# One level of Strassen's algorithm in the output projection of a hybrid decoder layer

## What is computed

```
h = rms_norm(x, norm_mix)
y_mix, xq = gla_branch(h, ...)                  # (2048, 1024), (2048, 512)
y_mem = memory_cross_attention(xq, m, w_kv)     # (2048, 512)
x = x + concatenate([y_mix, y_mem], -1) @ w_out # w_out is (1536, 1024): the product that is changed
x = x + (relu(rms_norm(x, norm_mlp) @ w_up) ** 2) @ w_down
return rms_norm(x, final_norm)
```

## Time and profile before

| what | value |
|---|---|
| median of 3 runs | 2588.22 us (2587.95 to 2590.2) |
| the profiled execution | 2587.02 us, of which the span in the trace is 2585.2 us |
| mean granted clock of PE | 0.998 of full |
| busy: PE, PEld | 2533.5 us (98%), 2118.9 us (82%) |
| busy: DVE, ACT, POOL | 1536.7 us (59%), 1205.3 us (47%), 452.9 us (18%) |
| DMA | 338.96 MB, mean 131 GB/s |

### The profile page before, as it was taken

The page is one execution under the profiler, slowest core; times in us unless marked ns, Lnnn a source line. Parts: engine busy times, 40 slices in busy tenths (PEclk is TensorE's granted clock), DMA queues, the critical chain, the costliest instruction groups (busy, mean ns, idle before and its releaser), DMA issues.

```text
span 2585.2 us, 34664 instructions
## 1 busy us (share of the span) xinstructions
PE 2533.5 (98%) x11968; PEld 2118.9 (82%) x11968; DVE 1536.7 (59%) x2253; ACT 1205.3 (47%) x1752; POOL 452.9 (18%) x411
## 2 busy tenths in 40 slices
PE   7999999999999999999999999999999999999998
PEld 6888887888788888888878888888887888888886
DVE  4457467665656636566646664656665565465666
ACT  4544344544454525455454443544445444354544
POOL 4144444000004510000001541000000254000000
PEclk9999999999999999999999999999999999999999
DMA  8522468444522132543442213255443222344443
GB/s 284 156 90 66 158 208 286 173 129 147 181 66 71 61 114 82 195 147 131 137 158 66 82 50 114 98 179 163 146 136 126 66 66 77 103 136 158 147 161 132
DMA packets 191896, 338.96 MB, mean 131 GB/s; under 512 B 7041, under 2 KB 119041, under 8 KB 183521
## 3 DMA queue, kind: packets, MB, share of 16 engines
q1 hardware_dynamic: 188784, 327.92, 38.3%
q10 hardware_dynamic: 2928, 8.66, 0.8%
HBM read 311.39 MB, written 25.17 MB: 130 GB/s over the span
## 4 chain that ended last, share of the span: by engine, by line
issue 49%; PE 40%; DVE 4%; POOL 4%; ACT 2%; DMA 1%; SPq 1%; DVEq 0%; ACTq 0%; POOLq 0%
PE banks L1593 10%; PE banks L1595 10%; PE banks L1594 10%; PE banks L1749 3%; PE banks L1729 1%; POOL queries L700 1%; DVE w_lo L1122 1%; POOL h_lo L725 1%; PE banks L1790 1%; PE banks L1773 1%; PE banks L1788 1%; POOL rstd L658 1%; DVE u_lo L1500 1%; ACT w_hi L761 1%; DVE sr L1332 0%
## 5 line engine op out<-in xcount | busy, mean ns | idle before, releaser
L1593 PE MATMUL banks<-h_hi,w_hi 128*128 128x512 f32 (+1 forms) x1728 | 667.5, 386 | 10.6 <-DVE w_lo L1122 3.6
L1595 PE MATMUL banks<-h_hi,w_lo 128*128 128x512 f32 (+1 forms) x1728 | 659.1, 381 | 0.0
L1594 PE MATMUL banks<-h_lo,w_hi 128*128 128x512 f32 (+1 forms) x1728 | 659.0, 381 | 0.0
L1122 DVE TENSOR_TENSOR w_lo<-raw,w_hi 128x2048 fp32r<-128x2048 f32 x144 | 349.2, 2425 | 297.7 <-ACT w_hi L761 297.7
L761 ACT ACTIVATE w_hi<-raw 128x2048 fp32r<-128x2048 f32 x144 | 275.5, 1913 | 269.6 <-PE banks L1593 230.1
L1593 PEld LDWEIGHTS banks<-h_hi,w_hi 128*128 128x128 f32 x1728 | 324.9, 188 | 77.1 <-issue 16.3
L1595 PEld LDWEIGHTS banks<-h_hi,w_lo 128*128 128x128 f32 x1728 | 324.8, 188 | 63.2
L1594 PEld LDWEIGHTS banks<-h_lo,w_hi 128*128 128x128 f32 x1728 | 325.0, 188 | 60.7
L1593 PE MATMUL banks<-w_hi,u_hi 128*128 128x512 f32 x896 | 351.8, 393 | 0.0
L1595 PE MATMUL banks<-w_hi,u_lo 128*128 128x512 f32 x896 | 349.1, 390 | 0.0
L1594 PE MATMUL banks<-w_lo,u_hi 128*128 128x512 f32 x896 | 348.8, 389 | 0.0
(11 more groups left out here) (170 smaller groups left out, 3224.3 us busy)
## 6 DMA issues: line engine op xcount, KB each, us to landing
raw<-in_w_up SPq DMA_DIRECT2D x64, 1024.0 KB, 5.4
raw<-w_mix SPq DMA_DIRECT2D x64, 1024.0 KB, 4.8
raw<-in_gla_w_in SPq DMA_DIRECT2D x57, 1024.0 KB, 5.0
raw<-in_w_down SPq DMA_DIRECT2D x48, 1024.0 KB, 4.7
raw<-in_w_out SPq DMA_DIRECT2D x24, 1024.0 KB, 5.0
xin<-in_x SPq DMA_DIRECT2D x5, 2048.0 KB, 10.9
xin<-in_w_down SPq DMA_DIRECT2D x10, 1024.0 KB, 4.9
w_mix<-xin SPq DMA_DIRECT2D x10, 1024.0 KB, 10.3
```

Source lines behind the costliest of these rows:

```text
L1122: nc.vector.tensor_tensor(w_lo[:, i % 2, :], raw[:, i % 2, :], w_hi[:, i % 2, :].bitcast(F32), ALU.subtract).then_inc(lo_split.sem, PIECES)
L1593: after_chunk(pe.matmul(to, left[0], right[0], start=start, stop=False, skip_group_check=goes_on))
L1594: pe.matmul(to, left[0], right[1], start=False, stop=False, skip_group_check=goes_on)
L1595: return pe.matmul(to, left[1], right[0], start=False, stop=stop, skip_group_check=goes_on)
```

## The change

The output projection of a block is written as the product of a left side of 512 tokens by 1536 and w_out, each cut in halves both ways. The inner halves are not contiguous: the first holds y's p = 0 and the memory's heads 0 and 1, the second y's p = 1 and heads 2 and 3. Seven products of 256 tokens (two pairs of tiles), 6 slices and 512 columns take the place of eight: 84 products a block. Each is cut into a part "m" (2 slices, memory) and a part "y" (4 slices):

```diff
-OUT_ORDER = (2, 0, 1)
-C_MLP = C_OUT + 6
+OUT_CHUNKS = [(("M1", "m"), ("M5", "m")), (("M1", "y"),), (("M2", "m"),), (("M2", "y"),), (("M5", "y"),),
+              (("M6", "m"),), (("M6", "y"),), (("M3", "m"), ("M7", "m")), (("M7", "y"),), (("M3", "y"),),
+              (("M4", "m"),), (("M4", "y"),)]
+C_MLP = C_OUT + len(OUT_CHUNKS)
...
+OUT_BANKS = {"M1": 2, "M6": 2, "M7": 2, "M4": 2, "M5": 4, "M3": 4, "M2": 6}
+ORDERED = {"M2": "M1", "M3": "M6", "M7": "M5"}
+Y_LOWS = [(0, 0), (1, 0), (0, 1), (1, 1), (2, 1), (3, 1)]
...
-MIX_STEPS = UPS
-MIX_EARLY = 6
-MIX_IN_OUT = 8
+OUT_MIX = 6
+MIX_STEPS = OUT_MIX + UPS
+MIX_EARLY = 9
+MIX_IN_OUT = 11
```

```diff
+                        C_OUT + 6: [(mix_load, 9), (mix_load, 10)], C_OUT + 9: [(mix_store, 9), (mix_load, 11)],
+                        C_OUT + 11: [(mix_store, 10), (mix_load, 12)], C_MLP: [(mix_store, 11), (mix_load, 13)],
...
-                    if i == C_OUT + 3:
+                    if i == C_OUT + 4:

                         sp.wait_ge(*read(n, ("oT", TILES - 1, 1)))
                         sp.dma_start(xres[:, :, :], x_tiles[:, bass.ds(x_row, TILES), :])\
```

The left sums of the memory's values are ten sums of 128x512 on POOL, one behind each of the half steps 5 to 14 of the recurrence. Those of y are four sums of 128x1024 on POOL, behind `su` of the last chunk, as their place in memory is that of the q and the states. ACT copies each sum to fp32r, DVE subtracts:

```diff
+            def mem_sums(n, step):
...
+                if behind is not None:
+                    pool.wait_ge(*mem_sum_step.at(n, behind))
+                nc.gpsimd.tensor_tensor(to, a, b, op).then_inc(mem_sum_step.sem, 1)
...
+                def y_sums():
...
+                    pool.wait_ge(*full(n, ("su", TILES - 1, 1)))
+                    nc.gpsimd.tensor_tensor(s3, a11, a21, ALU.subtract).then_inc(y_sum_ready.sem, 1)
+                    pool.wait_ge(*read(n, ("oT", TILES - 1, 1)))
+                    nc.gpsimd.tensor_tensor(s1, a21, a22, ALU.add).then_inc(y_sum_ready.sem, 1)
+                    pool.wait_ge(*y_sum_ready.at(n, 1))
+                    nc.gpsimd.tensor_tensor(s2, s1, a11, ALU.subtract).then_inc(y_sum_ready.sem, 1)
+                    pool.wait_ge(*y_sum_ready.at(n, 2))
+                    nc.gpsimd.tensor_tensor(s4, a12, s2, ALU.subtract).then_inc(y_sum_ready.sem, 1)
...
                 end_products(n, TILES - 1)
                 o_rsqrt(TILES - 1)
-                for p in range(2):
-                    for c in range(TILES):
-                        y_low(c, p)
+                for c, p in Y_LOWS[:4]:
+                    y_low(c, p)
+                y_sums()
+                for c, p in Y_LOWS[4:]:
+                    y_low(c, p)
```

DVE's order in the stage (`y_sum_low(S1)` waits for the sum S2 as well, since it writes over what S2 reads):

```diff
+                for c, p in Y_LOWS[2:4]:
+                    gate_output(c, p)
                 next_chunk(C_OUT + 1)
+                for c in (2, 3):
+                    for p in range(2):
+                        gate_output(c, p)
                 update_state(TILES - 1)
-                for c in range(TILES):
-                    gate_output(c, 1)
+                mem_sum_low(S4)
+                mem_sum_low(S3)
...
+                next_chunk(C_OUT + 2)
+                y_sum_low(S1)
+                next_chunk(C_OUT + 3)
+                y_sum_low(S2)
+                dve.wait_ge(*xres_loaded.at(n, 0))
+                add_product("M1")
+                y_sum_low(S4)
+                next_chunk(C_OUT + 4)
+                add_product("M2")
+                y_sum_low(S3)
+                next_chunk(C_OUT + 5)
+                add_product("M5")
...
+                add_product("M3")
+                split_lo_piece(n, C_OUT + 11, 1)
+                for t in range(2):
+                    norm_ms(0, t)
+                for t in range(2):
+                    norm_scale(0, t, xres, hn)
+                next_chunk(C_OUT + 11)
+                add_product("M4", (0,))
+                norm_ms(0, 2)
                 h_low(0, 0)
+                add_product("M4", (1,))
```

PE's order. M1 and M5 "m" are out_part(C_OUT, 0) and (C_OUT, 1):

```diff
+                out_part(C_OUT, 0)
+                pieces_done[0] = 1
+                output_transposes(0, 0)
+                output_transposes(1, 0)
+                out_part(C_OUT, 1)
+                pieces_done[0] = 1
                 state_step("o", TILES - 1)
+                output_transposes(0, 1)
+                output_transposes(1, 1)
+                out_part(C_OUT + 1, 0)
+                pieces_done[0] = 1
+                output_transposes(2, 0)
+                output_transposes(2, 1)
+                out_part(C_OUT + 1, 1, (0,))
+                output_transposes(3, 0)
+                output_transposes(3, 1)
+                out_part(C_OUT + 1, 1, (1,))
+                pieces_done[0] = 1
                 state_step("kT", TILES - 1)
+                out_chunk(C_OUT + 2)
                 state_step("su", TILES - 1)
...
+                for i in range(C_OUT + 3, C_MLP - 1):
+                    out_chunk(i)
```

More of the change, by code:

```diff
@@ L256, in state_uses @@
         for p in range(2):
-            yield (6 + p if last else 3 - p), ("su", c, p)
+            yield (p if last else 3 - p), ("su", c, p)
     elif what == "o":
@@ L515, in y_row, with row_of, out_piece_of, is_half @@
             return scratch[:, c, :] if c < 2 else y_rows[:, c - 2, :]
+        def row_of(c, p):
+            return late_rows[:, c, :] if p else y_row(c)
+        def out_piece_of(i, piece):
+            parts = OUT_CHUNKS[i - C_OUT]
+            name, part = parts[piece] if len(parts) > 1 else parts[0]
+            return name, part, 2 * piece if part == "y" else 0
+        def is_half(i):
+            return C_OUT <= i < C_MLP and OUT_CHUNKS[i - C_OUT][0][1] == "m" and len(OUT_CHUNKS[i - C_OUT]) == 1
+        def out_source(name, part):
+            operand = OPERANDS_OF[name][1]
+            if operand >= T1:
+                return w_out_mix[:, operand - T1, 0:4, :] if part == "y" else w_out_mix[:, operand - T1, 4:6, :]
+            row, col = {B11: (0, 0), B21: (1, 0), B22: (1, 1)}[operand]
+            first, count = (4 * row, 4) if part == "y" else (KD + 2 * row, 2)
+            return wout[:, first:first + count, 512 * col:512 * (col + 1)]
         def last_piece(i):
@@ L590, in load_block @@
             def load_block(n, x_row, x_next, first):
                 for i in range(1, C_MLP):
-                    load(n, i, chunk_source(i), KD if i < C_V or C_R <= i < C_OUT else KG)
-                    if i == C_OUT + 3:
+                    if i == C_OUT:
+                        for slot in range(3):
+                            sp.wait_ge(mix_stored[slot], 16 * sum(mix_slot(j) == slot for j in range(OUT_MIX)))
+                    if i < C_OUT:
+                        load(n, i, chunk_source(i), KD if i < C_V or C_R <= i else KG)
+                    else:
+                        load_out(n, i)
@@ L595, in load_block @@
+                    if i == C_OUT + 6 and first:
+                        sp.wait_ge(*read(n, ("su", TILES - 1, 1)))
+                    if i == C_OUT + 4:
                         sp.wait_ge(*read(n, ("oT", TILES - 1, 1)))
@@ L618, in load_block @@
                         for slot in range(3, 5):
-                            made = sum(mix_slot(j) == slot for j in range(DEPTH * (MLP[s][1] + 1)))
+                            made = sum(mix_slot(j) == slot for j in range(OUT_MIX + DEPTH * (MLP[s][1] + 1)))
                             if made:
```

377 lines of the change are left out of this document (276 added, 101 removed).

## The result

The changed kernel takes 2680.9 us (median of 4 runs, 2679.06 to 2682.93), the kernel before 2588.4 beside it: a ratio of 1.036, with a 95% interval of 1.034 to 1.037. The forecast was 2639 and the range ended at 2662, so the sign was right and the size too small by 42 us. The profiled execution took 2679.06 us, its span is 2677.3.

What follows compares the result with a forecast made beforehand. PE, 98% busy at full clock, was taken to bound the kernel. 2587.0 us plus 46.5 for four blocks (waits less saved matmuls) plus 5 for block 0 gave 2638.5, stated as 2639; range 2600 to 2662, at 0.8.

Steps and rivals of the forecast that it cites:

- (g): Block 0: three more mixing steps, and SP's queue standing for store landings ahead of chunk loads; 5 us, 0 to 20.
- The block's sum: All added waits of a block, 19.8 us, less 8.2 us of removed matmuls: +11.6 us a block, +46.5 over four.
- the saving: Output projection: 12 of 96 products a block removed, 36 matmuls at 0.227 us, 8.2 us a block.
- (a): Start of the output projection: PE waits 0.9 us for a bank at the second tile's transposes, behind DVE's last silu.
- (b): Before the first product's y part: PE waits 2.9 us for POOL's y_low, which stands behind the last chunk's o_rsqrt.
- (c): Behind su: PE waits 9.9 us for DVE's weight pieces, in turns with POOL's y sums; about 5 without turns, upper end 11.
- (d): Later in the output projection: DVE has no slack, PE waits 1.0 and 0.8 us before the sixth product's parts; 0 to 3.
- (e): End of the output stage: PE waits for the norm and first h_low of tiles 2 and 3, 1.8 us more; 0 to 4.
- (f): Recurrence, half steps 5 to 14: one more POOL sum each delays DVE's gaps and PE; 3.2 us a block, 0 to 4.5.
- The third rival: SP's blocked queue in block 0 costs the upper end of (g), beside the mixing: 2654 us; chance 0.15.
- The first (no turns): POOL's sums and DVE's splits hardly hold each other up: +2.5 us a block, 2602 us; chance 0.2.
- The second (waits under 8.2 a block): PE does not wait for the sums behind su, so the change wins: -5.1 us a block, 2567 us; chance 0.1.

## Why the prediction fell short, step by step

The step that failed is (g), block 0's mixing steps in SyncE's queue: put at 5 us, it took 46, and that is 41 of the 42 us between 2639 and 2680.9. A second miss, the clock behind a wait, had no term at all and was hidden by luck.

**The block's sum was right, its terms were not.** Predicted +11.6 a block, measured 11.5. But the waits were put at 19.8 and came to 15.4 of idle PE, and the saving was put at 8.2 and came to 3.9. Two misses of 4.4 and 4.3 us cancelled: that the sum came out is luck. PE's waits of block 1 in the kernel after, in time order:

```profile
880.60 1.75 PE L2022 MATMUL banks<-queries,keys 128*128 128x192 f32 x8 [2.58 <-POOL queries L837]
904.26 1.54 PE L2022 MATMUL banks<-queries,keys 128*128 128x192 f32 x8 [1.04 <-POOL queries L837]
918.26 0.65 PE L2034 MATMUL banks<-ident,k 128*128 128x128 f32 x4 [0.49 <-DVE inner_state L1590]
...
977.77 0.80 PE L1866 MATMUL banks<-w_hi,h_hi 128*128 128x512 f32 x1 [2.59 <-POOL h_lo L862]
1000.98 0.76 PE L1866 MATMUL banks<-w_hi,h_hi 128*128 128x512 f32 x1 [9.35 <-DVE w_lo L1341]
...
1049.71 0.38 PE L1866 MATMUL banks<-h_hi,w_hi 128*128 128x256 f32 x1 [1.44 <-DVE h_lo L1693]
1051.68 0.39 PE L1866 MATMUL banks<-h_hi,w_hi 128*128 128x256 f32 x1 [0.28 <-DVE h_lo L1693]
```

(a) 0.9 predicted, 0.6 measured. (b) 2.9, measured 2.59, by POOL's h_lo behind `o_rstd`, as walked.

(c) 9.9, measured 9.35, and no wait for piece 1. The mechanism is in the two queues, answering to the earlier trace rows. DVE, then POOL:

```profile
990.80 1.73 DVE L1590 SCALAR_TENSOR_TENSOR carried_state<-inner_state,chunk_decay,banks 128x256 f32<-128x256 f32 x4 [4.59 <-PE banks L2046]
992.46 4.89 DVE L1616 TENSOR_TENSOR mem_sum_lo<-mem_sum,mem_hi_b 128x512 fp32r<-128x512 f32 x2
997.27 6.67 DVE L1341 TENSOR_TENSOR w_lo<-raw,w_hi 128x1024 fp32r<-128x1024 f32 x2
...
991.71 2.34 POOL L873 TENSOR_TENSOR y_sum<-scratch,y_rows 128x1024 f32<-128x1024 f32 x1 [9.29 <-DVE carried_state L1590]
994.01 2.78 POOL L875 TENSOR_TENSOR y_sum<-y_rows,late_rows 128x1024 f32<-128x1024 f32 x1
996.88 2.67 POOL L877 TENSOR_TENSOR y_sum<-y_sum,scratch 128x1024 f32<-128x1024 f32 x1
999.62 3.23 POOL L879 TENSOR_TENSOR y_sum<-late_rows,y_sum 128x1024 f32<-128x1024 f32 x1
```

A sum of 1024 columns takes 2.34 us (2.4 taken). Two lows of 0.6 take 4.89 us, two pieces of 1.2 take 6.67, and POOL's sums 2.7 to 3.2. The rule of the Trainium skill, page "SBUF — State Buffer", section "Who interferes with whom", that a VectorE instruction with two SBUF inputs and a GpSimd one shut each other out, held here to 0.5 us of the sum; the run without y sums bears it out, as its longest wait is 3.8.

(d) 1.8 predicted, nothing measured. PE itself ran at half clock behind the wait, as the windows above show, which gives DVE time to catch up; that this is the reason was not tried apart. (e) 1.8, measured 1.44 + 0.28 = 1.7 against 0.75 before, so 1.0 more, not 1.8. (f) 3.2, measured 0.25 + 2.58 + 1.04 + 0.49 = 4.4 against 1.8 before: 2.6.

**The saving is where the first miss lies.** The sum took every wait at its own length and every matmul at 0.227 us. Behind the waits the granted clock fell to 1.2 GHz and matmuls ran at half speed; that is 3.4 of the missing 4.3 us a block, and 14.6 in the first. The earlier trace rows has the clock at full over a kernel whose PE hardly waits, but a row that told of it was at hand, far from the block that was walked. Near its start the kernel before has a wait of 2.26 us, and its clock falls right behind (the second line with the columns of the block table):

```profile
34.75 0.36 PE L1593 MATMUL banks<-w_hi,mem_hi 128*128 128x256 f32 x1 [2.26 <-DVE vm L1189]
36.00:38.00 2.00, 2.00 (x12) 2.00 (x11) 0.76 (x1) 1.14 (x1) 1.92 (x3) 0.55 1.08 386
```

The Trainium skill, page "TensorE: Matmul & The Clock Gate", section "HAM oscillation — how this bites in real kernels", says that a wait of TensorE in mid-kernel can throttle it, so that the work behind starts at the low clock and each such wait costs again; the rows agree. The prediction had waits of 9.4 and 2.9 us in its walk and gave them no such term. The two pauses put into the kernel before measure it: 1.7 us beyond a wait of 3.1 where the clock falls, 0.3 where it does not, and 3.2 a block, on average, beyond one of 9.8.

**(g) is the larger miss.** 5 us predicted, 20 at most; measured 38.7 in the first block and, by the run with fewer steps, 8.3 ahead of it. What the blocks leave of 92.1 us is 46 in all. The early steps were taken as hidden by POOL's idle time, and by that run they are not. The step named the right queue: loads of chunks behind a store's landing. It went wrong in the size, since it priced the three added steps by the mean of the ten there were (5.7 us for 10), and a mean taken where the queue has room says nothing of a queue that is full. The window 460 to 500 us of the kernel before, then of the kernel after:

```profile
460.00:500.00 40.00, 40.00 (x178) 33.11 (x177) 24.97 (x32) 23.43 (x30) 0.00 (x0) 1.00 0.36 124
```

```profile
460.00:500.00 40.00, 33.15 (x143) 26.28 (x142) 25.52 (x26) 10.14 (x10) 15.45 (x11) 1.00 0.81 282
```

Before, POOL has no more sums by then, the DMAs move 124 GB/s, and PE is busy all the time. With 13 steps the DMAs move 239 to 282 GB/s from 380 to 500, and every chunk's load has to stand in one line with stores that take 10.8 us to land. The experiments give the parts: the three steps 27 (with their spacing), the list's order 21, the bytes of the loads 16, the sums 3. They overlap and add up to more than 38.7, as each of them makes room in the same queue. The third rival, a blocked queue in the first block, was the right mechanism, priced at less than half of what it took.

**The rivals.** The first (no turns) fell with the 9.35 us. The second (waits under 8.2 a block) fell too: 15.4 us more of idle PE. Reordering brings that to 7.6, under its 8.2, and the later blocks to 633.0; they are still 2.8 over before's 630.2, because 3.4 of the 8.2 saved are missing in the busy time (4.8 less). Half clock makes 1.3 of these 3.4 there; the rest is not traced.

## What to carry to other kernels

Where PE is 98% busy, a change that saves matmuls pays with each wait that it makes, and for waits of the lengths seen here (2.3 to 9.8 us) a term belongs in the sum for the work that is done at half clock behind them (here up to 1.7 us behind 3.1, and 3.2 behind 9.8). Look for such a wait in the whole trace, not only in the block that you walk. Price added steps in a queue by walking the queue through its fullest stretch, each issue with what it waits for, never by the mean cost of the steps that fit before. And don't let one queue issue a store and right behind it the load into the same slot: a load that stood one chunk behind gave 21 us here for nothing.

## What the runs showed of the hardware that was not expected

- The clock behind a short wait differs in the same place: behind 3.12 us of waiting a matmul took 0.47 us in one block and 0.76 in the next. What decides it isn't settled by these runs. The Trainium skill, page "TensorE: Matmul & The Clock Gate", Part 1, calls the number of slow matmuls at a kernel's start "run-variable"; here the slow matmuls behind a wait varied within one run.
- Half clock also lay on the work right behind the wait: 11 matmuls in 4 us, granted clock 0.50, in the kernel before with the long pause.
- A 1 MB store landed in 10.8 us (median) from SyncE's queue and in 5.0 us from POOL's, in the same stretch of the kernel; it did not make the kernel faster (2678.1 us). With the loads a chunk behind, the stores from SyncE's queue landed in 7.1 us, so it isn't the queue alone.
- The turns fall unevenly on the two engines: DVE's pieces went from 1.2 to 3.3 us each, POOL's sums from 2.34 us to between 2.7 and 3.2.
